# Block 2's attentions: the score products of two heads issued back to back, once in two rounds

## What is computed

```python
def sparse_indexed_attention(q, k, v, q_idx, k_idx, w_idx):      # attention 0
    ...
        score = einsum('bqh,bqhs->bqs', wb, relu(logits)) * INDEX_SCALE
        _, sel = lax.top_k(score, top_k)
    ...
        s = einsum('bqhd,bqkd->bqhk', qb, kg) * (HEAD_DIM ** -0.5)
        p = softmax(where(valid, s, -inf))
        return einsum('bqhk,bqkd->bqhd', p, vg)

def chunked_band_attention(q, k, v, rel_bias):                   # attention 1
    ...
        s = einsum('bqhd,bkhd->bhqk', qc, kb) * (HEAD_DIM ** -0.5) + bias
        p = softmax(where(valid, s, -inf))
        return einsum('bhqk,bkhd->bqhd', p, vb)
```

## Time and profile before

| | us |
|---|---|
| median of 3 runs (4496.9 to 4510.25) | 4503.64 |
| the profiled execution | 4502.43 |
| its span, first to last instruction | 4500.6 |
| block 2, layer 0: attention 0, attention 1 | 119.6, 87.2 |
| block 2, layer 1: attention 0, attention 1 | 122.6, 87.2 |

### The profile page before, as it was taken

One profiled execution on the slowest core, in us unless ns is written; L12 is line 12 of the kernel. 1 busy time (PEld: TensorE's weight loads), 2 busy tenths in 40 slices (PEclk: granted clock), 3 DMA queues, 4 the chain that ended last, 5 costly groups with the idle time before them and its releaser, 6 DMA issues.

```text
span 4500.6 us, 67045 instructions
## 1 busy us (share of the span) xinstructions
PE 4071.0 (90%) x28912; PEld 3195.5 (71%) x28912; DVE 1462.2 (32%) x2700; ACT 1447.4 (32%) x2491; POOL 1382.6 (31%) x583
## 2 busy tenths in 40 slices
PE   7898889999988987899899698998999698998999
PEld 5687568777866875688778475676887465686887
DVE  4443341411144533413211356214111274213112
ACT  3343152223223441522222322433222332433222
POOL 4000314444430003244444142123444141133443
PEclk9899899999988997999999798899999796999999
DMA  3001112232210002122222323222222323122222
GB/s 127 2 3 40 59 61 94 75 114 94 94 65 11 3 8 87 47 94 94 98 94 94 140 75 115 91 73 91 94 94 94 130 86 140 48 94 75 94 94 94
DMA packets 26926, 357.88 MB, mean 80 GB/s; under 512 B 3216, under 2 KB 3344, under 8 KB 4368
## 3 DMA queue, kind: packets, MB, share of 16 engines
q1 hardware_dynamic: 23040, 329.26, 19.8%
q10 hardware_dynamic: 3600, 24.37, 1.4%
HBM read 351.52 MB, written 2.10 MB: 79 GB/s over the span
## 4 chain that ended last, share of the span: by engine, by line
PE 80%; DVE 11%; ACT 4%; issue 2%; DMA 2%; POOL 1%; ACTq 0%; SPq 0%; DVEq 0%; PEldq 0%; POOLq 0%; PEld 0%
PE bank L658 20%; PE bank L659 20%; PE bank L660 20%; PE bank L987 11%; PE bank L1936 5%; ACT arena L2095 2%; DMA ring<-stream 1%; PE bank L1962 1%; DVE arena L2389 1%; PE bank L2040 1%; DVE arena L2388 1%; ACT arena L1317 1%; DVE arena L1733 1%; DVE arena L1636 1%; POOL ring_r L746 1%
## 5 line engine op out<-in xcount | busy, mean ns | idle before, releaser
L746 POOL TENSOR_TENSOR ring_r<-ring,hi_ring 128x1024 fp32r<-128x1024 f32 (+1 forms) x522 | 1269.0, 2435 | 2613.8 <-ACT hi_ring L737 2613.7
L658 PE MATMUL bank<-xT_r,ring_r 128*128 128x512 f32 x2288 | 917.9, 401 | 23.5 <-DVE x_lo_r L2457 17.3
L659 PE MATMUL bank<-x_lo_r,hi_ring 128*128 128x512 f32 x2288 | 910.1, 398 | 0.0
L660 PE MATMUL bank<-xT_r,hi_ring 128*128 128x512 f32 x2288 | 906.4, 396 | 0.0
L737 ACT ACTIVATE hi_ring<-ring 128x1024 fp32r<-128x1024 f32 (+1 forms) x522 | 542.9, 1046 | 670.8 <-PE bank L660 358.6
L658 PEld LDWEIGHTS bank<-xT_r,ring_r 128*128 128x128 f32 x2288 | 438.8, 192 | 132.1 <-issue 31.0
L660 PEld LDWEIGHTS bank<-xT_r,hi_ring 128*128 128x128 f32 x2288 | 436.3, 191 | 102.3
L659 PEld LDWEIGHTS bank<-x_lo_r,hi_ring 128*128 128x128 f32 x2288 | 437.8, 191 | 97.4 <-issue 2.1
L987 PE MATMUL bank<-arena 64*64 64x64 f32 (+4 forms) x7456 | 395.3, 249 | 78.2 <-DVE arena L1636 29.6
L1317 ACT ACTIVATE arena<-bank 128x512 f32<-128x512 f32 (+1 forms) x422 | 230.6, 548 | 686.2 <-PE bank L660 479.4
L987 PEld LDWEIGHTS bank<-arena 64*64 64x64 f32 (+2 forms) x7456 | 305.2, 140 | 135.0 <-issue 92.1
(11 more groups left out here) (244 smaller groups left out, 4953.0 us busy)
## 6 DMA issues: line engine op xcount, KB each, us to landing
ring<-stream SPq DMA_DIRECT2D x156, 2048.0 KB, 7.7
arena<-ln_rows ACTq DMA_DIRECT2D x5, 1024.0 KB, 8.0
arena<-edge ACTq DMA_DIRECT2D x4, 1024.0 KB, 6.5
arena<-edge ACTq DMA_DIRECT2D x2, 1792.0 KB, 7.5
arena<-pack ACTq DMA_DIRECT2D x2, 1540.0 KB, 7.5
arena<-pack ACTq DMA_DIRECT2D x2, 1200.5 KB, 14.4
x<-x_in SPq DMA_DIRECT2D x4, 512.0 KB, 7.4
arena<-pack ACTq DMA_DIRECT2D x2, 1024.0 KB, 6.5
```

The source lines that it names most:

```text
L658: first = nc.tensor.matmul(out_, left[1], right[0], start=start, stop=False)
L659: low = nc.tensor.matmul(out_, left[0], right[1], start=False, stop=False)
L660: return first, low, nc.tensor.matmul(out_, left[0], right[0], start=False, stop=stop)
L746: nc.gpsimd.tensor_tensor(feed.raw(n, ring_r), feed.raw(n), feed.hi(n).bitcast(F32), ALU.subtract).then_inc(split_lo, 1)
```

## The change

The score products leave the head of each round. Heads 0 and 1 are issued ahead of round 0; then, at the end of each odd round n, after `s_pv` of head n - 3, those of heads n + 1 and n + 2 follow one another. `s_out` and `s_turn` stand behind them in the same round. Banks, waits and the arithmetic are the same; the other engines keep their order.

```diff
     def attend(a):
-        add("s_qk", a, 0, banks=(2,))
+        for n in range(2):
+            add("s_qk", a, n, banks=(2 + n,))
         for n in range(TT * HQ + 3):
-            if n + 1 < TT * HQ:
-                add("s_qk", a, n + 1, banks=(2 + (n + 1) % 2,))
             if n < TT * HQ:
                 add("s_soft", a, n)
...
             if n >= 3:
                 add("s_pv", a, n - 3)
+            if n % 2 and n + 1 < TT * HQ:
+                for m in (n + 1, n + 2):
+                    add("s_qk", a, m, banks=(2 + m % 2,))
             qt, h = divmod(n - 2, HQ)
```

## The result

The changed kernel takes **4467.8 us** (median of 4 runs, 4464.51 to 4470.12), beside 4506.94 (4 runs, 4496.9 to 4515.48) for the kernel before on the same chip: ratio 0.9913, 95% interval 0.9891 to 0.9936. It is faster by 0.9%. Every ratio here compares executions at the usual speed alone: one of only0 (6744.6 us) and one of samehalf (11531.7 us) stand far outside and are left out of theirs. The profiled execution of after took 4470.12, span 4468.3; its engines executed the same 67045 instructions.

A forecast was written before the change was run, and what follows sets the result against it. PE was taken to bound the four attentions (busy 386.1 of 416.6 us). Attention 1 gives 8 us, attention 0 13.6 and 13 in the two layers: 34.6 off 4502.4, so 4468 us, own range 4455 to 4484.

The forecast's parts named there:

- The pair is free: Score products on opposite row halves: the second costs nothing, saving 0.42, 0.63, 0.84, 1.05 us by width if nothing waited.
- The loop: Pair, maximum, exponential, copy, `s_pv`, next pair: period 4.36 us at width 512, so a pair saves 0.6, not 1.15.
- Attention 1, its start: Up to the second gate: 1.2 us from the first gate's wait, 2.0 from three pairs of 128 and one of 256.
- the first rival: Clock falls in attention 1's middle because of new waits: 10.5 us for each layer, 4489 us in all; chance 0.20.
- the rest: Rival, clock falls wherever it is full: 10 us more for each layer in attention 1; 4539 us in all; chance 0.08.
- Attention 0's wait in round 7: Transpose and unit of weights run during head 8's 4.46 us wait for VectorE (`head_scale`): gain 4.1 us in layer 0.
- Attention 0, the other stretches: Layer 0, from each `modulate` to the next: gains of 2.0, none, 2.4, 3.4, 1.25 and 0.45 us.
- No loop: Rival: the chain through ScalarE is not in PE's way, so the full saving counts: 4440 us; chance 0.11.
- no overlap: Rival: halves don't overlap in a pair; attention 1 loses 7 us for each layer, 4510 us in all; chance 0.07.

The follow-up runs named there:

- only0: New order in attention 0 alone, attention 1 in the old order, against the kernel before: 4454.2 us, ratio 0.9883.
- samehalf: The changed kernel with every score product reading the lower row half, so a pair has no two halves: 4491.2 us, ratio 0.9966 against the kernel before.
- mid0: New order in attention 0 alone, its pair just ahead of `s_pv` instead of behind it; attention 1 in the old order: 4447.3 us, ratio 0.9888 against before.
- fill1: New order in attention 1 alone, plus products nobody reads where PE waits for ScalarE's copy there: 4495.9 us, ratio 0.9990 against the kernel before.
- only1: New order in attention 1 alone, attention 0 in the old order, against the kernel before: 4523.4 us, ratio 1.0038.
- midboth: The changed kernel with the pair just ahead of `s_pv` of its round in both attentions: 4447.7 us, ratio 0.9866 against the kernel before.
- midfill: midboth plus the unread filler products of fill1 in attention 1: 4457.1 us, ratio 0.9888 against the kernel before.
- fillboth: midfill with fillers in attention 0 too, and one filler of 512 in place of two in attention 1: 4431.5 us, ratio 0.9853 against the kernel before.

## Why the prediction was right

The time was 4468 forecast and 4467.8 measured. The direction and the pair's price were right for the reasons given; that the two times agree to 0.2 us is luck. The terms compare so:

- **The pair is free.** Right at all four widths: a pair takes the 0.42, 0.63, 0.85 and 1.06 us of a lone product, so 0.84 for 384 and 0.42 for 128 were well chosen. What was missed is that 0.2 us of each is saved by standing together and not by the halves.
- **The loop.** Right in place and size from width 256 up: 4.44 for 4.36, 2.87 for 2.8, 3.65 for 3.6, each 0.05 to 0.08 over. Between gates 12.50 and 15.73 us at full clock, for 12.3 and 15.4; from the fourth gate to the last wait 14.95 for 14.6. Small as these are, they take the whole forecast of 0.85 us for the three stretches: 0.2 and 0.3 gained, 0.5 lost. The waits are those named: 0.74 and 0.43 once in two rounds, 1.82 behind `s_turn`.
- **Attention 1, its start: the step that failed.** Forecast 3.2 us of the 4 for each layer, with three pairs of 128 counted as a gain. The prediction has the chain at 128, 1.75, but sets no period against it as it does at 256 and above. At equal clock the pairs lose, as the two orders show at width 128 (mid0 with the old order, then fill1, both at 1.00):

```profile
2862.86 0.75 PE L1940 MATMUL bank<-arena 128*128 128x64 f32 x4
...
2864.55 0.96 PE L1940 MATMUL bank<-arena 128*128 128x64 f32 x4
```
```profile
2890.73 0.83 PE L1942 MATMUL bank<-arena 128*128 128x64 f32 x6 [0.30 <-ACT arena L2106]
...
2893.22 0.86 PE L1942 MATMUL bank<-arena 128*128 128x64 f32 x6 [0.69 <-ACT arena L2106]
...
2894.11 0.29 DVE L2424 CUSTOM_DVE_ANT_0 arena<-bank,arena 128x128 f32<-128x128 f32 x1 [1.18 <-PE bank L1942]
...
2894.63 0.40 ACT L2106 ACTIVATE arena<-arena,small 128x128 f32<-128x128 f32 x1 [0.92 <-DVE small L2427]
...
2895.03 0.26 ACT L2106 ACTIVATE arena<-bank 128x128 f32<-128x128 f32 x1
...
2895.34 1.07 PE L1942 MATMUL bank<-arena 128*128 128x64 f32 x6 [0.28 <-ACT arena L2106]
```

  Two rounds take 1.69 in the old order, and 2.49 and 2.12 in the new one. The second loop is the plain one: the pair starts at 2893.59 inside its row, the `s_pv` at 2895.34, so the chain is 1.75 exactly as forecast, and the `s_pv` ahead of the pair adds 0.37. That is 2.12 against 1.69. The first is longer because VectorE fills a border of the bias (L2419 there, 0.33 us) ahead of its maximum. Between the first and second gate the pairs lose 0.6 us (7.82 against 7.18), and with the 1.3 us gained ahead of the first gate and the other stretches attention 1 at full clock is 80.0 against 80.6. **At full clock the change is worth 0.6 us there, not 4.** That after shows 1.3 and 4.2 less than before is the clock of before: 0.66 in this part, 10.1 us for what takes 7.18 at full clock, and two gates of 7.3 and 7.2 us that take 5.6 to 5.7 at full clock.
- **The clock in attention 1, the first rival.** It came in part: in layer 0 the third gate is at 0.79 and the stretch behind it at 0.90, 2.9 us, with 0.3 more just ahead of them; behind the second gate layer 1 has none of it. In both layers the first part is low too, 0.71 and 0.80 between the first and second gate, and that is the other 2.3 and 2.5 us by which 85.4 and 82.5 exceed 80.0. In only1 it came whole, 12.3 us for each layer, against 10.5 priced for the middle alone and 20 with the rest. The Trainium skill, "TensorE: Matmul & The Clock Gate", "A second HAM failure mode: psum-queue depth-cycling", says that frequent short idles between groups of products make the clock swing and cost throughput. The trace agrees in only1 and fill1 (0.82 to 0.85 with the waits, 1.00 with the waits filled), and after's layer 1, with the same waits at 1.00 behind the second gate, shows that it need not come.
- **Attention 0's wait in round 7.** Right: the short products start 19.0 us after the attention's start, 23.0 before, so 4.0 for the 4.1 forecast. The step missed what it gives back, 2.3 in the next stretch, where I had counted a gain of 2.0: that stretch became 0.5 longer (14.24 to 14.78).
- **Attention 0, the other stretches.** Forecast 9.5 for layer 0; they gave 14.4 (18.4 less the 4.0). The surplus is one stretch, from the fifth unit of weights to the sixth, forecast 3.4, measured 8.5; the others miss in both directions, from 2.5 less than forecast to 1.5 more, and come out even. First before, then after:

```profile
2821.50:2841.30 19.80, 18.98 (x73) 11.03 (x72) 3.33 (x15) 5.85 (x16) 0.00 (x0) 0.59 0.42 160
```
```profile
2818.63:2829.93 11.30, 9.47 (x74) 6.37 (x73) 4.73 (x20) 4.80 (x14) 0.00 (x0) 1.00 0.57 216
```

  Nearly the same records (one score product of 512 in before is one of 384 in after) take 18.98 us of PE at a clock of 0.59 and 9.47 at 1.00. Length times clock is 11.7 us before and 11.3 after, so the 8.5 us are nearly all clock. I had doubled the products for the half clock and kept the clock. samehalf, in which the products of a pair don't overlap, has the same stretch at 12.0 us and 0.95 in layer 0 and at 16.4 and 0.71 in layer 1. Over all kernels the old order of attention 0 takes 19.5 to 22.0 us here (before, only1, fill1, both layers) and the new orders 10.3 to 16.4, so the order brings it and not the overlap alone. How much it brings isn't certain: layer 1 of after reads 12.85 at 0.77, midboth 15.4 at 0.67. Why the clock is granted there is open.

So three misses cancel: attention 1 gave 5.5 in place of 8 (and that by the clock of its start), attention 0 38.0 in place of 26.6, and the parts that don't change took back 11.3 in this execution. The four attentions gave 43.5 us where 34.6 were forecast. "No loop" at 4440 and "no overlap" at 4510 are out, by the waits and by samehalf's pairs rather than by the time.

## What to carry to other kernels

Two half-row products side by side halve their time, but an order that puts them together also moves what waits for them: write out the chain from the pair through the other engines' queues back to TensorE at the narrowest width too, since there the chain shrinks less than TensorE's work (3.42 to 1.75 us here, against 4.96 to 1.69 for two rounds). Put the pair ahead of work that is already ready (here `s_pv` of its round), not at the round's end. And where the new order leaves short waits, compare at equal granted clock before judging it; a product that nothing reads, put into the wait, shows what the clock costs and can be left in as the cure.

## What the runs showed of the hardware

- The granted clock is the larger term of both signs. Attention 1 in its old order took 86.7 us at a clock of 0.92 in before and 80.6 at 1.00 in mid0, and in pairs 92.3 at 0.84 in only1 and, with fillers added, 80.0 at 1.00 in fill1.
- It falls behind waits, yet not always. After has the same `s_pv` and pair behind the same wait in both layers, at half clock in one and at full clock in the other:

```profile
2916.94 3.22 PE L1938 MATMUL bank<-arena 128*128 128x64 f32 x10 [1.91 <-ACT arena L2097]
...
3887.17 1.94 PE L1938 MATMUL bank<-arena 128*128 128x64 f32 x10 [1.91 <-ACT arena L2097]
```

  What tells the two apart is open. And it was low without any wait: the earlier trace rows, and 18.98 of 19.80 us busy at 0.59.
- Fillers in PE's waits went with a clock of 1.00 in attention 1 in fill1, midfill and fillboth, in each of the six attentions seen. In attention 0 they raised the clock from 0.83 to 0.90 and 0.92 only.
- Two products that stand together cost 0.2 us less than two apart even on the same half; on opposite halves the second costs nothing (0.42 to 1.06 us a pair against 0.64 to 1.91).
